# Expert layer of a two-block transformer: the first 64 tokens take picked rows by indirect DMA, the other 448 stay dense

## The reference, cut to what matters

```python
def peer(h, w_pq, sub_keys, u_emb, v_emb):
    q = (h @ w_pq).reshape(B, S, PEER_HEADS, 2, PEER_DHALF)          # 8 heads
    sc = einsum("bshcd,hcnd->bshcn", q, sub_keys)                    # 2 x 128 scores a head
    s_top, i_top = top_k(sc, 16)
    cand = s_top[..., 0, :, None] + s_top[..., 1, None, :]           # 16 x 16 sums
    best, pos = top_k(cand, 16)                                      # 16 experts a head
    gate = softmax(best)
    a = gelu(einsum("ced,cd->ce", u_emb[idx], hx))                   # 128 experts a token
    return einsum("ce,ced->cd", g * a, v_emb[idx])
```

## Time and profile before

| what | value |
|---|---|
| time, median of 3 runs | 3474.71 us (3473.66 to 3476.45) |
| span of the profiled execution | 3474.6 us |
| TensorE busy | 3425.9 us, 99% |
| VectorE busy | 1991.5 us, 57% |
| ScalarE busy | 1258.6 us, 36% |
| GpSimd busy | 903.0 us, 26% |
| granted TensorE clock, mean | 0.998 of full speed |

### The profile page before, as it was taken

One profiled execution on the slowest core, in us unless ns is written; L12 is line 12 of the kernel. 1 busy time (PEld: TensorE's weight loads), 2 busy tenths in 40 slices (PEclk: granted clock), 3 DMA queues, 4 the chain that ended last, 5 costly groups with the idle time before them and its releaser, 6 DMA issues.

```text
span 3474.6 us, 43049 instructions
## 1 busy us (share of the span) xinstructions
PE 3425.9 (99%) x16522; PEld 2791.9 (80%) x16530; DVE 1991.5 (57%) x3136; ACT 1258.6 (36%) x1848; POOL 903.0 (26%) x379
## 2 busy tenths in 40 slices
PE   7999999999999999999999999999999999999998
PEld 5877788888888888888888887888768888888886
DVE  7899769788888886322222226320568765632205
ACT  3334533223333333322222224332345656333215
POOL 0010243441000000444444443444121000444432
PEclk9999999999999999999999999999999999999999
DMA  3211233333565456555555552222322222322222
GB/s 124 94 52 44 102 103 122 122 122 128 176 206 171 167 174 217 205 194 194 194 194 194 194 194 91 97 97 97 117 66 76 72 79 73 122 97 97 97 97 85
DMA packets 144167, 447.27 MB, mean 129 GB/s; under 512 B 12840, under 2 KB 45992, under 8 KB 139744
## 3 DMA queue, kind: packets, MB, share of 16 engines
q1 hardware_dynamic: 107968, 405.26, 34.1%
q10 hardware_dynamic: 36000, 39.27, 3.2%
HBM read 373.16 MB, written 71.32 MB: 128 GB/s over the span
## 4 chain that ended last, share of the span: by engine, by line
PE 86%; DVE 8%; DVEq 3%; ACT 1%; issue 1%; DMA 1%; POOL 0%; SPq 0%; ACTq 0%; POOLq 0%
PE ps L207 53%; PE ps L1053 20%; PE ps L1360 6%; PE ps L1036 3%; DVE conv_out L755 2%; PE ps L2367 1%; DVEq L742 1%; PE ps L1637 1%; DVE m_gates L2116 1%; PE ps L1581 1%; PE ps L1723 1%; PE ps L1706 0%; DVE norm_r L279 0%; DVEq L817 0%; DVE x_low L259 0%
## 5 line engine op out<-in xcount | busy, mean ns | idle before, releaser
L207 PE MATMUL ps<-h_norm_hi,slot_parts 128*128 128x512 f32 x4576 | 1457.8, 395 | 10.9 <-DVE x_low L237 6.7
L195 POOL TENSOR_TENSOR slot_parts<-ring,slot_parts 128x1024 fp32r<-128x1024 f32 x362 | 880.8, 2434 | 2254.0 <-ACT slot_parts L191 2254.0
L207 PEld LDWEIGHTS ps<-h_norm_hi,slot_parts 128*128 128x128 f32 x4576 | 859.4, 188 | 204.9 <-issue 9.1
L207 PE MATMUL ps<-x_low,slot_parts 128*128 128x512 f32 x2224 | 864.9, 389 | 0.0
L191 ACT ACTIVATE slot_parts<-ring 128x1024 fp32r<-128x1024 f32 x560 | 589.3, 1053 | 473.7 <-DMA ring<-in_stream 305.1
L1053 PE MATMUL ps<-gated_hi,slot_parts 128*128 128x512 f32 x2048 | 630.9, 389 | 0.3 <-DVE slot_parts L195 0.3
L207 PEld LDWEIGHTS ps<-x_low,slot_parts 128*128 128x128 f32 x2224 | 418.7, 188 | 86.9
L1053 PEld LDWEIGHTS ps<-gated_hi,slot_parts 128*128 128x128 f32 x2048 | 384.4, 188 | 80.6 <-DVE slot_parts L195 0.8
L195 DVE TENSOR_TENSOR slot_parts<-ring,slot_parts 128x1024 fp32r<-128x1024 f32 x198 | 242.8, 1226 | 357.2 <-ACT slot_parts L191 352.0
L1053 PE MATMUL ps<-gated_lo,slot_parts 128*128 128x512 f32 x1024 | 398.4, 389 | 0.0
L1286 DVE TENSOR_TENSOR gated<-gates_back,experts_back 128x512 f32<-128x512 f32 x128 | 93.4, 730 | 498.8 <-DMA experts_back<-experts_dram 479.3
(11 more groups left out here) (407 smaller groups left out, 3495.6 us busy)
## 6 DMA issues: line engine op xcount, KB each, us to landing
ring<-in_stream SPq DMA_DIRECT2D x560, 512.0 KB, 3.3
experts_dram<-experts SPq DMA_DIRECT2D x64, 512.0 KB, 4.7
gates_dram<-gates_by_key ACTq DMA_DIRECT2D x32, 1024.0 KB, 10.8
gates_back<-gates_dram SPq DMA_DIRECT2D x32, 1024.0 KB, 4.8
experts_back<-experts_dram SPq DMA_DIRECT2D x64, 512.0 KB, 5.2
x_res<-in_xT SPq DMA_DIRECT2D x4, 512.0 KB, 8.1
x_res<-in_xT SPq DMA_DIRECT2D x1, 2048.0 KB, 8.4
x_dram<-x_res SPq DMA_DIRECT2D x4, 512.0 KB, 3.3
```

What stands on the lines that cost most here:

```text
L195: e.tensor_tensor(to[:, BUFFER[n], 1, :], ring[:, n % RING, :], to[:, BUFFER[n], 0, :].bitcast(F32), ALU.subtract).then_inc(s_lo, 1)
L207: mm = e.matmul(psum, w2[wv][:, k, :], x2[xv], start=start and v == 0, stop=stop and v == 2)
```

## The change

For the first 64 tokens (`LONE`) the experts are no longer computed densely. Their 64 x 128 = 8192 picks are laid out as 64 steps (`STEPS`) of 128 rows: partitions 0 to 63 hold the first 64 picks of the 64 tokens, partitions 64 to 127 the other 64.

- All u matmuls, v matmuls, Gelu copies, gate products and one-hot groups cover 448 tokens (`SD`): 448 columns instead of 512, 112 groups instead of 128, seven blocks instead of eight in `W_dram`. The query slots keep 512 columns.
- **At the turn** DVE computes row indices (`pick_tab`), a folding matrix and `h` twice over; ACT moves half of the table by a DMA; TensorE turns `h` (8 transposes after slot j = 38), ACT copies it to `h_rows`.
- **u rows, beside the dense u stretch.** POOL issues one indirect DMA of 128 rows of 4 KB for each step into four buffers and multiplies the rows by `h_rows` (128x1024); ACT sums each product (`accum_out`), step s placed after slot j = 48 + 78 s / 64 or so. One Gelu at the end.
- **v rows, beside the dense v stretch.** POOL issues a second indirect DMA for each step into six buffers (six before the stretch, the others after its `slot_lo` calls); DVE adds gate times row into `row_sum` (one scalar_tensor_tensor of 128x1024 for each step).
- Before the last three v slots TensorE adds `row_sum` through the folding matrix into columns 0 to 63 of each bank (8 small matmuls).

```diff
+LONE, ROWS_U, ROWS_V = 64, 4, 6
+SD, STEPS = S - LONE, S // 8
...
-    GROUPS = S // WT
+    GROUPS = SD // WT
...
+    DOTS_FROM, SUMS_FROM, SUMS_TO = TURN + 12, 4, NKEY - TAIL - 4
+    def dots_after(j):
+        n = NKEY - 2 - DOTS_FROM
+        return range(*[max(0, min(STEPS, STEPS * (x - DOTS_FROM) // n)) for x in (j, j + 1)])
+    def sums_after(j):
+        n = SUMS_TO - SUMS_FROM
+        return range(*[max(0, min(STEPS, STEPS * (x - SUMS_FROM) // n)) for x in (j, j + 1)])
...  # peer_pe
+            ts = slice(LONE if kind == "u" else 0, S)
-                mm = product3(e, PS[:, i % 2, :], w2, k, (x2[0][:, k, :], x2[1][:, k, :]), k == 0, k == KT - 1)
+                mm = product3(e, PS[:, i % 2, ts], w2, k, (x2[0][:, k, ts], x2[1][:, k, ts]), k == 0, k == KT - 1)
+            if kind == "u" and j == TURN + 2:
+                e.wait_ge(r_h, R_ONCE + 1)
+                for k in range(KT):
+                    mm = e.transpose(PS[:, 2 + k // 4, k % 4 * P:(k % 4 + 1) * P], row_0[:, k * P:(k + 1) * P], ident)
+                mm.then_inc(r_turned, 1)
...
+            if len(js) > 1:
+                e.wait_ge(r_sum, R_MANY + STEPS)
+                for d in range(KT):
+                    e.matmul(PS[:, d, 0:LONE], row_sum[:, d * P:(d + 1) * P], fold[:, :], start=False, stop=False)
...
-                    mm = e.matmul(PS[:, d, :], w2[wv][:, d * P:(d + 1) * P], g_[xv],
+                    mm = e.matmul(PS[:, d, LONE:], w2[wv][:, d * P:(d + 1) * P], g_[xv],
...  # peer_act, at the end of each slot of BEFORE_V
+                for s in dots_after(j):
+                    e.wait_ge(r_mul, R_MANY + s + 1)
+                    e.activation(u_rows[s % ROWS_U], u_rows[s % ROWS_U], ACT.Copy, accum_out=row_dot[:, s:s + 1])\
+                        .then_inc(r_dot, 1)
+        e.wait_ge(r_dot, R_MANY + STEPS)
+        e.activation(row_act[:, :], row_dot[:, :], ACT.Gelu).then_inc(r_dot, 1)
...  # peer_pool
+        e.wait_ge(r_half, R_HALF + 16)
+        e.wait_ge(w_hot, 1)
+        e.wait_ge(r_rows, R_ONCE + 1)
+        def u_row(s):
+            after(e, r_dot, R_MANY + s - ROWS_U + 1 if s >= ROWS_U else 0)
+            e.indirect_dma_start(u_rows[s % ROWS_U], None, a["peer_u"], pick(0, s)).then_inc(ru_in[s % ROWS_U], 16)
+        def v_row(s):
+            after(e, r_sum, R_MANY + s - ROWS_V + 1 if s >= ROWS_V else 0)
+            e.indirect_dma_start(v_rows[s % ROWS_V][:, :], None, experts_v, pick(1, s))\
+                .then_inc(rv_in[s % ROWS_V], 16)
+        for s in range(ROWS_U - 1):
+            u_row(s)
+        for s in range(STEPS):
+            e.wait_ge(ru_in[s % ROWS_U], 16 * (s // ROWS_U + 1))
+            e.tensor_tensor(u_rows[s % ROWS_U], u_rows[s % ROWS_U], h_rows[:, :], ALU.mult).then_inc(r_mul, 1)
+            if s + ROWS_U - 1 < STEPS:
+                u_row(s + ROWS_U - 1)
...
+            for s in sums_after(n - n_v - 1):
+                if s + ROWS_V < STEPS:
+                    v_row(s + ROWS_V)
...  # peer_dve, after the last gate step, before the copies of the turned tables
+        key1, key2, gate = (T[0:LONE, x, 0, :] for x in range(3))
+        at = pick_at[0:LONE, :]
+        e.tensor_scalar(at, key2, float(NKEY), float(n_v * NKEY), ALU.mult, ALU.add)
+        e.drain()
+        for half, to in enumerate((pick_tab, pick_tmp)):
+            ...
+        e.tensor_tensor(fold[:, :], ident[:, 0:LONE], ident[:, LONE:], ALU.add)
+        for x in range(2):
+            ins = e.tensor_tensor(h_twice[:, :, x, :], Hh[:, :, 0:LONE].bitcast(F32), Lo[:, :, 0:LONE].bitcast(F32),
+                                  ALU.add)
...  # peer_dve, v stretch
+                for s in sums_after(j):
+                    e.drain()
+                    e.wait_ge(rv_in[s % ROWS_V], RV_IN[s % ROWS_V] + 16 * (s // ROWS_V + 1))
+                    ...
+                        e.scalar_tensor_tensor(out=row_sum[:, :], in0=v_rows[s % ROWS_V][:, :],
+                                               scalar=row_gate[:, s:s + 1], in1=row_sum[:, :], op0=ALU.mult,
+                                               op1=ALU.add).then_inc(r_sum, 1)
```

More of the change, by code:

```diff
@@ L921, in build @@
     m = ExitStack()
+    BLOCKS = SD // WBLK
     keep(m, 2)
@@ L973, in build @@
     a_in = [sem(f"experts_in{i}") for i in range(2)]
+    r_tab, r_h, r_turned, r_rows = ln_in, ln_mu, ln_mm, ln_root
+    R_ONCE = 1
+    r_mul, r_dot, r_sum = ln_xc, ln_sq, ln_sum
+    R_MANY = KT
+    r_half, R_HALF = m1_pos, 16
+    rv_in = [sem(f"expert_row{x_}") for x_ in range(ROWS_V)]
+    ru_in, RV_IN = rv_in[:ROWS_U], [16 * (STEPS // ROWS_U) * (x_ < ROWS_U) for x_ in range(ROWS_V)]
     v_g, v_hi, v_lo, v_out, v_add = sems("v_", "gated", "gated_hi", "gated_lo", "out", "added")
     n_p, n_v = START["peer_heads"], START["peer_v"]
+    experts_v = a["stream"].rearrange("n p c -> (n p) c")
     BEFORE_V = []
@@ L1071, in first_u @@
             e.wait_ge(n_inv, 3 + j)
-            e.activation(A[:, 0, j, :], u_raw[:, j, :], ACT.Gelu).then_inc(p_ev, 1)
+            e.activation(A[:, 0, j, :], u_raw[:, j, LONE:], ACT.Gelu).then_inc(p_ev, 1)
         e.wait_ge(n_mm, 2 * KT)
@@ L1097, in peer_act @@
                     after(e, a_out[j // 2 % 2], 16 * (j // 4))
-                e.activation(A[:, j // 2 % 2, j % 2, :], PS[:, i % 2, :], ACT.Gelu).then_inc(p_ev, 1)
+                e.activation(A[:, j // 2 % 2, j % 2, :], PS[:, i % 2, LONE:], ACT.Gelu).then_inc(p_ev, 1)
             slot_hi(e, n_p + i + 2)
+            if kind == "u" and j == TURN:
+                e.wait_ge(r_tab, R_ONCE + 1)
+                e.dma_start(pick_tab[LONE:, :, :], pick_tmp[0:LONE, :, :]).then_inc(r_half, 16)
+            if kind == "u" and j == TURN + 3:
+                e.wait_ge(r_turned, R_ONCE + 1)
+                e.activation(h_rows[:, :], PS[:, 2:4, :].rearrange("p a s -> p (a s)"), ACT.Copy).then_inc(r_rows, 1)
             if i == len(BEFORE_V) - 2:
@@ L1138, in peer_pool, with pick @@
             slot_lo(e, n)
+        e.wait_ge(r_half, R_HALF + 16)
+        e.wait_ge(w_hot, 1)
+        e.wait_ge(r_rows, R_ONCE + 1)
+        def pick(table, s):
+            return bass.IndirectOffsetOnAxis(ap=pick_tab[:, table, s:s + 1].bitcast(U32), axis=0)
+        def u_row(s):
[12 more added lines that the diff above has]
+                u_row(s + ROWS_U - 1)
+        for b in range(2):
+            e.wait_ge(w_out[b], 64 * ((BLOCKS + 1 - b) // 2))
+        for s in range(ROWS_V):
+            v_row(s)
         e.wait_ge(s_lo, ORDINAL[n_v])
@@ L1180, in first_slot @@
             e.wait_ge(slot_done, n_p + i + 1)
-            e.tensor_tensor(to, PS[:, i % 2, :], norm_r[:, :], ALU.mult).then_inc(done, 1)
+            ts = slice(LONE if i > 1 else 0, S)
+            e.tensor_tensor(to[:, ts], PS[:, i % 2, ts], norm_r[:, ts], ALU.mult).then_inc(done, 1)
         first_slot(0, qh[:, 0, :], p_ev)
@@ L1502, in build @@
     x_dram = nc.dram_tensor("x_dram", (P, KT, S), F32, kind="Internal").ap()
-    b_mm, b_row, b_dram = sems("bias_", "product", "rows", "dram")
-    m2_in, m2_hd, m2_iw, m2_qk, m2_v, m2_wide, m2_spill = sems(
-        "m2_", "in", "evac", "iw", "qk", "v", "wide", "spill")
+    b_dram = sem("bias_dram")
+    b_mm, b_row, i_ax, B_MM, B_ROW, I_AX = k_cos, m1_trig, m1_ang, 2, 2, 2
+    m2_iw, i_alo, M2_IW, I_ALO = m1_zero, v_done, 1, 1
+    m2_in, m2_hd, m2_qk, m2_v, m2_wide, m2_spill = sems(
+        "m2_", "in", "evac", "qk", "v", "wide", "spill")
     m2_back = [sem(f"m2_x_back{i}") for i in range(2)]
@@ L1565, in mixer2_pe @@
             if t == 0:
-                e.wait_ge(i_alo, 1)
+                e.wait_ge(i_alo, I_ALO + 1)
             after(e, m2_qk, t - 3)
             if t == 1:
-                e.wait_ge(b_row, 2)
-                e.wait_ge(m2_iw, 1)
+                e.wait_ge(b_row, B_ROW + 2)
+                e.wait_ge(m2_iw, M2_IW + 1)
             for k in range(KT):
```

70 lines of the change are left out of this document (50 added, 20 removed).

## The result

The changed kernel takes 3448.53 us (median of 4 runs, 3445.55 to 3452.74) where the kernel before takes 3474.85 on the same chip: ratio 0.9925, 95% interval 0.9911 to 0.9939. So it is 26 us faster (0.75%, clear of the noise of these runs), where 66 were forecast. The profiled execution has a span of 3450.9 us.

A forecast was written before the change was run, and what follows sets the result against it. TensorE bounds the kernel now, VectorE the u stretch after the change. From 3474.6 us, -23.7 + 4.5 + 37 - 4.5 - 82.0 + 1 + 2 = -65.7 gives 3409 us; own range 3385 to 3440, 8 in 10 3380 to 3500.

The forecast's parts named there:

- VectorE became the bound of the u stretch: Slots 37 to 120: VectorE needs 591 us, TensorE 487, so the stretch takes 592 us, 37 more than before.
- an exclusion with GpSimd: U stretch: each GpSimd product stops VectorE for 2.19 us, 62 of them 136 us; the rival of no exclusion, 3304 us, 6%.
- the gathers cost next to nothing: U stretch: issuing a gather on GpSimd takes nothing from VectorE; the rival that gathers shut out more got 15%.
- the weight load does not bind: Matmuls at 448 columns reach 0.200 to 0.202 us; the rival, a load holding 0.227 to 0.229 and 3519 us, 5%.
- the v stretch stays TensorE's: VectorE and GpSimd need 4.0 us of a 4.84 us slot, so 3072 matmuls gain 82.0 us, some 615 us in all.
- gathers with a small price: U stretch: each of 62 gather issues also shuts VectorE out for 0.3 to 1 us, giving 3428 to 3471 us; chance 8%.
- the turn: Between heads and u stretch: TensorE arrives earlier and waits for VectorE's chain and new index work; 4.5 us lost.
- the slots before it: 37 u slots before the turn: 888 matmuls at 0.0267 us less each gain 23.7 us; query slots unchanged.
- slots 121 to 127: End of the u matmuls, without groups: they go at TensorE's pace, 168 x 0.0267 = 4.5 us gained.
- if that part stays, 64 columns less are worth 0.0267 us: All narrowed matmuls: the 0.0135 to 0.016 us beside the columns stays constant; 0.0285 if all is in proportion.
- keep some slack: Before the turn: VectorE's work for a head hides under its 6 slots (32.97 us) with time left.
- collisions of POOL with DVE in the heads at another phase: Heads before the turn: up to 10 us more, counted in the forecast's own range only.

The follow-up runs named there:

- dve_products: The changed kernel with its 64 products issued on VectorE, behind the one-hots of their slot, instead of on GpSimd: 3369.12 us, ratio 0.969.
- widths: The kernel before with its v matmuls cut in steps of 16 slots, from 512 down to 256 columns, left-out columns not computed: 3375.95 us in one run.
- dense_only: The changed kernel without gathers, products, sums and their waits, so the first 64 tokens lack their experts: 3321.56 us, ratio 0.956.
- products_16: The changed kernel with each GpSimd product cut from 1024 to 16 elements, gathers, sums and v rows kept: 3335.88 us, ratio 0.9601.

## Why the prediction was right in direction and wrong in size

Right: VectorE became the bound of the u stretch, by an exclusion with GpSimd that is read from the earlier trace rows and paid once for each product; the gathers cost next to nothing; the weight load does not bind; the v stretch stays TensorE's. The time lies in the range of 3380 to 3500, but above the 3385 to 3440 that the prediction gave its own mechanism. It lies where the prediction had put gathers with a small price (3428 to 3471), which the runs refute; that the wide range holds it is partly luck.

The mechanism held and sizes failed: five terms of the sum make up the 40 us. The two large ones are the v stretch (18 us; the saving per column taken as constant, and one pace taken for granted) and VectorE's time in the u stretch (15.6 us; the price of a product and VectorE's own need). The others are the turn (3.4), the slots before it (2.8) and slots 121 to 127 (1.7).

**The u stretch, VectorE's side: +52.6 us, forecast +37.** Two sizes. The exclusion costs 2.36 us for a product where I took 2.19, the stretching of one instruction in the earlier trace rows; the upper bound that the prediction kept, GpSimd's own 2.40, was the truer price (62 x 0.17 = 10.5 us). And VectorE's own need is 461, not 455 (6 us): 112 groups and 84 `slot_lo` at their best spacing leave out its waits for ScalarE's halves, 2.9 us in dve_products, from which the 461 are worked out; the rest of the 6 was not traced. In the changed kernel these waits are 11.0 us, so some 8 us of what is priced here as exclusion are waits: the stretched instructions alone give 2.3 us a product.

**The v stretch: -61 us, forecast -79.** The step that failed is "if that part stays, 64 columns less are worth 0.0267 us". It does not stay. At 0.0240 (run widths) 3072 matmuls save 73.7 us instead of 82.0, and dense_only has this: 697 - 625 = 72, with its fold of 1.8 us. Another 11 us go beyond dense_only: 7.7 with the slow pace (642 of 1024 intervals at 0.62 instead of 0.608) and 3.4 with a few short waits, where the prediction had 2 for the start. The exclusion does stretch VectorE's instructions here too, but VectorE is busy 382 of 636 us and the buffers cover it; that was forecast.

**The turn: 7.9 us, forecast 4.5 (bounds 1 and 9).** TensorE comes to it 20.9 us earlier, after 36 slots that are each 0.64 us shorter (5.50 and 4.86) less 1.6 of waits for slot parts near their start and 0.4 that I did not trace; the column there was worth what I took. The 23.7 forecast are 2.8 more; they also count slot 36, which stands behind the turn. Then it waits:

```profile
789.78 2.61 PE L1038 MATMUL ps<-squares_const,picks 128*128 128x128 f32 x11 [6.45 <-DVE picks L1337]
```

I had let VectorE's work for a head "keep some slack". Before it had 5.5 us: a head costs VectorE 29.26 us where it does not wait (586.04 to 615.30), and TensorE gives it a new one each 34.76. After the change it has none. These are the lines of a head that now collide with GpSimd:

```profile
588.45 2.73 DVE L1323 TENSOR_TENSOR row_hot<-row_hot,top_index_f 128x1024 bf16<-128x1024 bf16 x1
...
604.46 2.46 DVE L1307 CAST top_index_f<-top_index 128x128 bf16<-128x128 uint32 x1
...
616.22 1.73 DVE L1313 TENSOR_SCALAR pos_row<-best_pos 128x64 uint32<-128x64 uint32 x1
...
620.66 2.73 DVE L1323 TENSOR_TENSOR row_hot<-row_hot,top_index_f 128x1024 bf16<-128x1024 bf16 x1
```

```profile
604.45 2.39 POOL L197 TENSOR_TENSOR slot_parts<-ring,slot_parts 128x1024 fp32r<-128x1024 f32 x1 [2.45 <-ACT slot_parts L193]
...
615.49 2.40 POOL L197 TENSOR_TENSOR slot_parts<-ring,slot_parts 128x1024 fp32r<-128x1024 f32 x1 [3.08 <-ACT slot_parts L193]
```

The CAST of L1307 takes 2.46 us (0.23 before), the TENSOR_SCALAR of L1313 1.73 (0.86 before), since GpSimd's `slot_lo` now comes at another moment of the head: 32.21 us from row_hot to row_hot. TensorE's own period is 32.21 as well (four slots of 448 columns, two of 512, the scores), so VectorE never catches up, does not wait for scores once (27.8 us in five waits before), and it comes to the row_hot near the end of its last head only 8.7 us earlier (780.39 against 789.07). dense_only has the same period (32.20 to 32.23 us), so this comes with the narrower slots and not with the sparse part. The wait is 6.45 of the 7.9 us; the new index work, forecast at 3.3 less 0.7, accounts for no more than the other 1.5, with TensorE's transposes at half of the clock behind the wait. The prediction had "collisions of POOL with DVE in the heads at another phase" as up to 10 us of its range, but put them at nothing in its sum. No run takes these collisions away; that they are the cause is read from these lines alone.

**Slots 121 to 127: 2.8 us less, forecast 4.5.** TensorE comes to them out of a wait at half of the clock: the `_lo` matmuls take 0.57 us at first and 0.37 from 1409.14 on.

The working of the sum, 2.8 (pace and first waits) + 3.4 (turn) + 15.6 + 1.7 + 18, gives 41.5 us, and 3409 + 41.5 = 3450.5, where the profiled execution took 3450.9; the second block has 0.3 us of the rest.

## What to carry to other kernels

Before work is given to an idle engine, look for one place in the trace where it already runs beside the engine that is nearly full: here one line of eight rows told that GpSimd's tensor_tensor costs VectorE its whole length, twice what VectorE would need to do it. Price such a collision at the intruder's duration, and place the work in the stage in which the engine that pays has time left: the same sums with products on VectorE, half of them in the v stretch, take 3341 us instead of 3449. And a saving per column, measured at one width, holds only roughly at another (in the v stretch 64 columns less saved 0.0240 us from 512 to 448, 0.0294 from 448 to 384), so a term of 3000 matmuls needs its bound.

## What the runs showed of the hardware

- The issue of a gather of 128 rows of 4 KB takes GpSimd 0.94 to 2.29 us (means of 1.40 to 1.75 us in the u stretch, 1.18 in the v stretch) and costs VectorE next to nothing: 2.2 us for all steps of products_16, and in dve_products its instructions keep their length beside them.
- GpSimd's tensor_tensor of 1024 elements costs VectorE 2.3 to 2.4 us, one of 512 elements 1.27, each about as long as it lasts itself. Beside it VectorE's tensor_tensor, CAST (0.23 to 2.46 us) and TENSOR_SCALAR (0.86 to 1.73) are stretched. The FIND_INDEX8 of a head on the scores in PSUM keep their 0.29 us beside it (596.11, with GpSimd busy from 594.74 to 597.14).
- The exclusion goes both ways a little: GpSimd's products take 2.54 to 2.80 us in the mean beside VectorE's one-hots, its `slot_lo` in dense_only 2.40.
- The same matmul of 448 columns has paces of 0.2027 and 0.2067 us, each held over 100 us and more at the same granted clock of 1.00; the cause is open.
- In the u stretch of the changed kernel, where TensorE waits up to 4.5 us at a time (70.0 us in 24 waits for the one-hots), the granted clock is 0.95 over the stretch and at its lower level, 1.2 GHz, for some 3 to 7 us at a time, each time behind a wait of 2.3 to 4.5 us; in both stages of dense_only, without such waits, it is 1.00.
